# Hybrid decoder trunk on one core: routing places taken per token row, another store order for the rows, and Abs_reciprocal_sqrt in the norms

## The reference

```
def _layer_norm(x, g, b):
    mu = mean(x);  var = mean((x - mu)**2)
    return (x - mu) * rsqrt(var + LN_EPS) * g + b
def _moe_ffn(h, ...):
    scores = sigmoid(h @ w_router);  biased = scores + router_bias      # 64 experts
    keep the 4 best of 8 groups (sum of each group's two best biased scores)
    idx = top_k(biased of the kept groups, 8)
    w = 2.5 * scores[idx] / sum(scores[idx])
    routed = sum over the 8 experts of w * (silu(h Wg) * (h Wu)) Wd
    return routed + shared expert
```

## Time and profile before

| | |
|---|---|
| runs | 1547.74, 1555.4, 1553.97 us; median 1553.97 |
| profiled execution | 1548.17 us; span 1546.3 us from the first to the last instruction |
| PE busy | 1439.7 us (93%) |
| DVE, ACT, POOL busy | 649.5 us, 342.0 us, 244.7 us |
| DMA | 512.37 MB, mean 331 GB/s |
| `norm_and_route` of layer 0, of layer 1 | from 383.9 us to about 411.5; from 1023.6 to about 1052.9 |
| `experts` of layer 0, of layer 1 | from 411.66 us to about 900; from 1053.06 to 1534.7 |

### The profile page before, as it was taken

How to read it: one execution, slowest core, us unless ns; L and a number is a source line. 1 busy time by engine, 2 the same in 40 slices (tenths; PEclk the granted TensorE clock), 3 DMA queues, 4 the chain that set the end, 5 groups by cost and what they waited for, 6 DMA issues and landing times. The chain is left out here.

```text
span 1546.3 us, 24294 instructions
## 1 busy us (share of the span) xinstructions
PE 1439.7 (93%) x9414; PEld 849.9 (55%) x9414; DVE 649.5 (42%) x1461; ACT 342.0 (22%) x712; POOL 244.7 (16%) x323
## 2 busy tenths in 40 slices
PE   8999989999899999897999889989999989979996
PEld 6888768887445545353545467864543333424442
DVE  2767448632632433242433358053234323414324
ACT  3756454220410111010111030141101111101111
POOL 5779625200100000000000000011000000000000
PEclk9999999899999999998999989999999999989998
DMA  8669461049599999999999973498999999999994
GB/s 282 218 190 243 174 173 47 2 164 365 208 417 422 423 420 424 424 421 425 421 425 421 409 281 129 169 392 336 417 424 423 421 425 422 425 421 424 422 423 183
DMA packets 105679, 512.37 MB, mean 331 GB/s; under 512 B 36932, under 2 KB 42116, under 8 KB 68444
## 3 DMA queue, kind: packets, MB, share of 16 engines
q1 hardware_dynamic: 95740, 481.75, 78.7%
q0 software_dynamic: 9824, 29.05, 5.0%
HBM read 508.85 MB, written 17.10 MB: 340 GB/s over the span
## 5 line engine op out<-in xcount | busy, mean ns | idle before, releaser
L1855 PE MATMUL banks<-upper,e_xgT 128*64 128x512 f32 (+1 forms) x880 | 195.1, 609 | 3.5 <-DMA upper<-in_moe_gate_up 2.1
L2064 DVE TENSOR_TENSOR e_ac<-e_sl,banks 128x256 f32<-128x256 f32 x54 | 22.8, 421 | 405.8 <-ACT e_sl L1982 405.8
L346 PE MATMUL banks<-hT,dense_ring 128*128 128x272 f32 x768 | 183.3, 396 | 5.3 <-DMA dense_ring<-in_w_in 5.2
L1444 POOL DMA_INDIRECT x_xg<-rows_dram,x_idx x54 | 53.8, 996 | 824.7 <-DVE x_idx L1436 808.6
L346 PEld LDWEIGHTS banks<-hT,dense_ring 128*128 128x128 f32 x768 | 145.8, 191 | 39.0 <-DMA dense_ring<-in_w_in 5.4
L1855 PE MATMUL banks<-dense_ring,e_xgT 128*64 128x512 f32 (+1 forms) x288 | 134.5, 622 | 34.7 <-issue 34.7
L1855 PE MATMUL banks<-experts,e_xgT 128*64 128x512 f32 (+1 forms) x720 | 159.3, 604 | 1.1 <-DMA experts<-in_moe_gate_up 0.9
L1982 ACT ACTIVATE e_sl<-banks 128x256 f32<-128x256 f32 x54 | 20.8, 385 | 491.2 <-PE banks L1855 491.2
L1855 PEld LDWEIGHTS banks<-upper,e_xgT 128*64 128x64 f32 (+1 forms) x880 | 65.0, 131 | 91.0 <-issue 91.0
L1875 PE MATMUL banks<-x_sg,route_consts 128*128 128x272 f32 x432 | 104.4, 393 | 0.5 <-DVE acc L2051 0.5
L1873 PE MATMUL banks<-route_consts,x_sg 128*128 128x512 f32 x216 | 97.6, 594 | 0.8 <-DVE acc L2048 0.8
(11 more groups left out here) (450 smaller groups left out, 2061.1 us busy)
## 6 DMA issues: line engine op xcount, KB each, us to landing
upper<-in_moe_gate_up SPq DMA_DIRECT2D x45, 2048.0 KB, 27.9
experts<-in_moe_gate_up SPq DMA_DIRECT2D x36, 2048.0 KB, 27.1
upper<-in_moe_down SPq DMA_DIRECT2D x43, 1024.0 KB, 25.5
experts<-in_moe_down SPq DMA_DIRECT2D x43, 1024.0 KB, 26.4
dense_ring<-in_moe_down SPq DMA_DIRECT2D x38, 1024.0 KB, 25.5
dense_ring<-in_moe_gate_up SPq DMA_DIRECT2D x18, 2048.0 KB, 19.1
dense_ring<-in_w_in SPq DMA_DIRECT2D x47, 512.0 KB, 4.8
upper<-in_moe_gate_up SPq DMA_DIRECT2D x20, 1024.0 KB, 15.0
```

Of the source, the lines that this page charges most:

```text
L346: mm = pe.matmul(ps[g % 4][:, 0:T], slot[:, n % SLOTS_IN, c, :], hT[:, c, :], start=(c == 0), stop=(c == DC - 1))
L1444: pool.indirect_dma_start(out=ex["xg"][:, i % 2, :], out_offset=None, in_=mem["rows_dram"], in_offset=bass.IndirectOffsetOnAxis(ap=ex["idx ...
L1855: mm = pe.matmul(gub[e * n:(e + 1) * n, :], xgT[:, i % 2, c, e * n:(e + 1) * n], gate_up_weights(mem, j)[:, c, :], start=(c == 0), stop=(c ...
L2064: dve.tensor_tensor(ac[:], sl[:], gub[:, FF:], ALU.mult).then_inc(mul, 1)
```

## The change

The edits, with what each does:

- In both norms the inverse root comes from one ACT function, `Abs_reciprocal_sqrt`, in place of `Sqrt` and DVE's reciprocal (routing) and of `Ln` and `Exp` (S5 stage). A one-element call of it stands at the start of ACT's list.
- POOL scales the router weights first and clears `x_xg` after the centring.
- ACT does only chunk 0 before the logits' `Sigmoid`, and seven after it.
- Rows are turned, copied and stored with the 16-row tile first (`turn_order`: 2, 0, 1 in layer 0; 0, 1 in layer 1).
- Places are formed by token: PE makes them from `after` and `sel` (six small products in layer 0, three in layer 1), DVE adds 1 and masks, PE turns them to expert rows. DVE takes the maximum from PSUM, ACT then copies the places.
- PE ranks before it spreads; places and gates are spread by separate products, the gates after the sort. DVE's selectors (`select_unit`) come before the scaling, the scatter after the order.

```
 def scalar(act):
+    act.activation(rstd[0:1, 0:1], eps[0:1, 2:3], ACT.Abs_reciprocal_sqrt).then_inc(held, 1)
     for c in range(DC):
         act.wait_ge(centred, c + 1)
         act.activation(sq[:, c, :], hN[:, c, :], ACT.Square).then_inc(squared, 1)
     act.wait_ge(sq_summed, 1)
-    act.activation(rstd[:], sqs[:, 0:T], ACT.Ln, scale=1.0 / D, bias=eps[:, 2:3]).then_inc(logged, 1)
-    act.wait_ge(logged, 1)
-    act.activation(rstd[:], rstd[:], ACT.Exp, scale=-0.5).then_inc(rooted, 1)
+    act.wait_ge(held, 1)
+    act.activation(rstd[:], sqs[:, 0:T], ACT.Abs_reciprocal_sqrt, scale=1.0 / D, bias=eps[:, 2:3]).then_inc(rooted, 1)
...
+turn_order = tuple(range(2, NT)) + (0, 1)
...
-        pool.memset(ex["xg"][:], 0.0).then_inc(ex["xg_zero"], 1)
         pool.wait_ge(loaded, 48 * (layer + 1))
         pool.tensor_tensor(wg[:], wr[:], ln[:, 4 * layer * DC:(4 * layer + 1) * DC].unsqueeze(2).broadcast_to(
             [P, DC, E]), ALU.mult).then_inc(weighed, 1)
-        for tt, (t0, n) in enumerate(tiles):
-            pool.wait_ge(rows_c, NT + tt + 1)
+        pool.wait_ge(centred, DC)
+        pool.memset(ex["xg"][:], 0.0).then_inc(ex["xg_zero"], 1)
+        for i, tt in enumerate(turn_order):
+            t0, n = tiles[tt]
+            pool.wait_ge(rows_c, NT + i + 1)
             pool.dma_start(mem["rows_dram"][t0:t0 + n, :], row_tile(tt)[0:n]).then_inc(stored, 16)
...
-            half, tt = divmod(i, NT)
+            half, tt = i // NT, turn_order[i % NT]
...
         pe.wait_ge(selected, 1)
         for tt, (t0, n) in enumerate(tiles):
-            mm = pe.matmul(rank_ps[0:E, 0:W], sel[0:n, tt, :], after[0:n, tt, 0:W],
-                           start=(tt == 0), stop=(tt == NT - 1))
+            for src, (_, held) in enumerate(tiles[:tt + 1]):
+                mm = pe.matmul(place_ps[0:n, tt * E:(tt + 1) * E], after[0:held, src, t0:t0 + n], sel[0:held, src, :],
+                               start=(src == 0), stop=(src == tt))
+        mm.then_inc(ranked, 1)
+        pe.wait_ge(located, 1)
+        for tt, (t0, n) in enumerate(tiles):
+            mm = pe.transpose(row_places_ps[0:E, t0:t0 + n], sel[0:n, tt, :], ident[0:n, 0:n])
         mm.then_inc(ranked, 1)
         pe.wait_ge(gated, 1)
...
-        pe.wait_ge(placed, 2)
-        pe.wait_ge(rows_c, 2 * NT)
-        for i in range(2):
-            spread_unit(pe, mem, ex, i, spread_ps[i], W)
         pe.wait_ge(mem["expert_consts"], 16 * len(EXPERT_CONSTS))
         pe.wait_ge(keyed, 1)
         pe.matmul(key_ps[0:E, 0:E], ones[0:E, 0:E], keys[:], start=True, stop=True).then_inc(spread, 1)
-        pe.wait_ge(masked, 1)
+        pe.wait_ge(placed, 1)
+        pe.wait_ge(rows_c, 2 * NT)
+        pe.wait_ge(ex["unit_selected"], 2)
+        for i in range(2):
+            pe.matmul(spread_ps[i][0][:, 0:W], ex["selw"][0:E, i], pg[0:E, 0:W], start=True, stop=True).then_inc(
+                ex["rows_broadcast"], 1)
+        pe.wait_ge(placed, 2)
         pe.wait_ge(placed_by, 2)
         pe.matmul(sort_ps[:, 2 * E:2 * E + 1], twice, rank[:], start=True, stop=True)
         pe.matmul(sort_ps[0:1, 0:E], number, at_rank[:], start=True, stop=True)
         pe.matmul(sort_ps[0:1, E:2 * E], cm[:], at_rank[:], start=True, stop=True).then_inc(sorted_, 1)
+        for i in range(2):
+            pe.matmul(spread_ps[i][1][:, 0:W], ex["selw"][E:, i], pg[E:, 0:W], start=True, stop=True).then_inc(
+                gates_spread, 1)
...
+        act.activation(warm[:], eps[0:1, 0:1], ACT.Abs_reciprocal_sqrt).then_inc(warmed, 1)
         for c in range(DC):
             act.wait_ge(centred, c + 1)
             act.activation(sq[:, c, :], hN[:, c, :], ACT.Square).then_inc(squared, 1)
         act.wait_ge(sq_summed, 1)
-        act.activation(rstd[:], sqs[:, 0:W], ACT.Sqrt, scale=1.0 / D, bias=eps[:, 2:3]).then_inc(sd_ready, 1)
-
+        act.activation(rstd[:], sqs[:, 0:W], ACT.Abs_reciprocal_sqrt, scale=1.0 / D, bias=eps[:, 2:3]).then_inc(rooted, 1)
+
+        act.wait_ge(warmed, 1)
         act.activation(warm[:], eps[0:1, 0:1], ACT.Sigmoid).then_inc(warmed, 1)
-        for c in range(3):
-            normal(c)
+        normal(0)
         act.wait_ge(logit_in, 1)
         act.wait_ge(bias_in, 1)
         act.activation(lgT[:], lgT[:], ACT.Sigmoid, bias=bias[:, 0:1]).then_inc(scored, 1)
-        for c in range(3, DC):
+        for c in range(1, DC):
...
-        act.wait_ge(ranked, 2)
-        act.copy(maskT[:], both_ps[0:E, 0:W]).then_inc(masked, 1)
+        act.wait_ge(counted, 1)
+        act.copy(pg[0:E, 0:W], row_places_ps[0:E, 0:W]).then_inc(placed, 1)
+        act.wait_ge(ranked, 3)
         act.copy(pg[E:, 0:W], both_ps[E:, 0:W]).then_inc(placed, 1)
         for i in range(2):
-            gates_in(act, ex, i, spread_ps[i], W)
+            act.wait_ge(gates_spread, i + 1)
+            act.copy(ex["gsb"][:, i], spread_ps[i][1][:, 0:W]).then_inc(ex["gates_in"], 1)
...
+        dve.wait_ge(mem["expert_consts"], 16 * len(EXPERT_CONSTS))
+        fixed = mem["unit_first"]
+        for i in range(2):
+            select_unit(dve, mem, ex, i, fixed[:, len(UNITS) + i:len(UNITS) + i + 1])
         dve.wait_ge(biased, 1)
         dve.tensor_copy(bias[:], bias_ps[0:E, 0:1]).then_inc(bias_in, 1)
-        dve.wait_ge(sd_ready, 1)
-        dve.reciprocal(rstd[:], rstd[:]).then_inc(rooted, 1)
         dve.wait_ge(rooted, 1)
...
+        dve.wait_ge(ranked, 1)
+        dve.scalar_tensor_tensor(out=sel, in0=place_ps[:, 0:NT * E].rearrange("p (t e) -> p t e", t=NT), scalar=1.0,
+                                 in1=sel, op0=ALU.add, op1=ALU.mult).then_inc(located, 1)
...
-        dve.wait_ge(mem["expert_consts"], 16 * len(EXPERT_CONSTS))
-        fixed = mem["unit_first"]
-        for i in range(2):
-            select_unit(dve, mem, ex, i, fixed[:, len(UNITS) + i:len(UNITS) + i + 1])
-        dve.wait_ge(masked, 1)
-
-        dve.scalar_tensor_tensor(out=pg[0:E, 0:W], in0=rank_ps[0:E, 0:W], scalar=1.0, in1=maskT[:],
-                                 op0=ALU.add, op1=ALU.mult).then_inc(placed, 1)
-        dve.wait_ge(placed, 2)
-        link(dve.tensor_reduce(cm[:], pg[0:E, 0:W], AX_X, ALU.max))
+        dve.wait_ge(ranked, 2)
+        dve.tensor_reduce(cm[:], row_places_ps[0:E, 0:W], AX_X, ALU.max).then_inc(counted, 1)
+        dve.wait_ge(counted, 1)
...
-        locate_unit(dve, mem, ex, 0, spread_ps[0], W)
         dve.wait_ge(spread, 1)
...
-        locate_unit(dve, mem, ex, 1, spread_ps[1], W)
         for i in range(2):
-            scatter_unit(dve, mem, ex, i, spread_ps[i], W)
-        link(dve.tensor_scalar(extra[:], rank[:], PAIR_RANKS - 0.5, float(SLOTS // 2), ALU.is_gt, ALU.mult))
+            locate_unit(dve, mem, ex, i, spread_ps[i], W)
         dve.wait_ge(sorted_, 1)
...
-        dve.wait_ge(ex["rows_broadcast"], 2)
-        link(dve.scalar_tensor_tensor(out=pg[0:E, 0:W], in0=maskT[:], scalar=extra[:, 0:1], in1=pg[0:E, 0:W],
-                                      op0=ALU.mult, op1=ALU.add))
+        dve.wait_ge(placed_by, 2)
+        link(dve.tensor_scalar(extra[:], rank[:], PAIR_RANKS - 0.5, float(SLOTS // 2), ALU.is_gt, ALU.mult))
+        link(dve.tensor_scalar(lifted[:], pg[0:E, 0:W], 0.0, extra[:, 0:1], ALU.is_gt, ALU.mult))
+        link(dve.tensor_tensor(pg[0:E, 0:W], pg[0:E, 0:W], lifted[:], ALU.add))
+        for i in range(2):
+            scatter_unit(dve, mem, ex, i, spread_ps[i], W)
```

More of the change, by code:

```diff
@@ L1288, in layer_norm @@
     sq, mean, rstd = sb("ln_sq", [P, DC, T]), sb("ln_mean", [P, T]), sb("ln_rstd", [P, T])
[L1289 to L1290 removed]
+    meaned, centred, squared, sq_summed, held, rooted, scaled, out = (sem(f"ln_{n}") for n in (
+        "meaned", "centred", "squared", "sq_summed", "table_held", "rooted", "scaled", "out"))
     def tensor(pe):
```

16 lines of the change are left out of this document (7 added, 9 removed).

## The result

Kernel after: 1558.05 us median (1552.7 to 1564.88, 9 runs); kernel before, run beside it: 1552.93 us (1547.74 to 1555.4, 9 runs). The ratio is 1.0037, 95% interval [1.0019, 1.0055]: slower by 5.7 us by the ratio (3 to 8.5); the two medians lie 5.1 apart. The forecast was +2.0 us, 1553.3 us in all. The profiled execution took 1558.05 us, its span is 1556.3 us, its mean granted clock 0.961 (0.968 in that of before).

What follows compares the result with a forecast made beforehand. The prediction took the weight stream's start to bound the experts, timed by ACT's rows in layer 0 and PE's chain in layer 1. Layer 0 +1.4, layer 1 +0.6, S5 norm 0: +2.0 on 1551.3 gives 1553.3 us, range 1545 to 1559.

Steps and rivals of the forecast that it cites:

- What bounds the kernel: Expert stages: weights stream at a constant rate, its start timed by ACT's row copies in layer 0, PE's chain in layer 1.
- no gap opens in layer 0: Layer 0's first unit: first two loads last 7.5 us, and the next are asked for halfway through that unit.
- Stream +1.4 us: Layer 0: later selection (0.4) and two moved Identities (1.05) delay last copy, gather and SP's first load by 1.4 us.
- The added table load: Start of ACT's list: 1.28 us, over inside DVE's standstill, so no cost; without that cover 0.5.
- The places' chain at full clock: Layer 0, from `sel` written: gates done at +6.6, shared product at +10.45, PE's first turn at +11.4 against +10.9.
- a clock of 0.5 there: Layer 0's routing: listed among the signs that would show the forecast wrong.
- rival B: Layer 0's clock falls as layer 1's did; first unit 3 us later, a gap opens, about +5, 1556.3 us; chance 0.12.
- forecast at the full clock: Layer 0: PE's first turn comes 0.5 + 0.4 = 0.9 us later, at 412.6.
- The gather's landing: Layer 0: gather moves with the last store and lands at PE's first turn or up to 0.3 us after.
- the sooner order: Layer 0: order known some 0.8 us sooner, which buys nothing while SP waits for the gather.
- Root, S5 norm, tiles first: Layer 0's reciprocal saves nothing; S5 root 1.75 us sooner, hidden by `s_wb`, gain 0; store order -0.4 to +0.3, taken as 0.
- Layer 1 +0.6: Layer 1: shared product starts 1.4 us later but runs less at half clock; +0.6 us, from -0.7 to +1.5.

Runs made afterwards that it cites:

- number 7: Kernel after with SP waiting for both gathers and, as in the kernel before, store order, Identities and POOL's list: 1554.54 us, ratio 1.0021.
- fillers and the wait: Kernel after plus 20 unused products of ones in PE's pauses per routing stage, and SP waiting for both first gathers: 1546.86 us, ratio 0.9963.
- all cures: Kernel after plus filler products, SP waiting for both gathers, three Identities ahead of the sigmoid and POOL's clearing first: 1548.1 us, ratio 0.9973.
- SP's second wait: Kernel after, but SP waits until both first gathers are issued, not one, before loading the first unit's weights: 1554.42 us, ratio 1.0013.
- number 3: Kernel after plus filler products of ones in PE's pauses of both routing stages, nothing else: 1560.59 us, ratio 1.0052.
- 4: Kernel after with SP waiting for both first gathers: alone 1554.42 us, ratio 1.0013; with filler products 1546.86 us, ratio 0.9963.
- number 8: Kernel before with POOL kept busy between the first index and the first gather, so the load follows the gather closely: 1562.68 us, ratio 1.0064.
- places alone: Kernel before with only the new chain of places; root, Identities, store order and POOL's clearing as before: 1555.92 us, ratio 1.0022.
- number 9: The failure: kernel after with fillers and the first unit's index taken ahead of the ranks, without SP's second wait: 1557.43 us, ratio 1.0043.

## Why the prediction was wrong, step by step

- **What bounds the kernel: wrong; this is the step that failed first.** "So layer 0's expert stage is timed by ACT's rows, not by the places", and "so no gap opens in layer 0". The stage is timed by PE's first turn, in layer 0 as in layer 1: from there layer 0 takes 488.0 to 490.5 us in 18 traces. That the DMA engines are never idle at 500 us says nothing of 420 us. The numbers were there: by my own sum the 3 MB were through at 410.3 + 7.5 = 417.8, and a third load as far behind the turn as before (5.8 us) came at 418.4. So I had called a path with no slack hidden, and entered layer 0 with the 1.4 us of ACT's rows in place of what the turn loses.
- **Stream +1.4 us: right for the copies, too much by half for the load, and without effect.** Copies end +1.56 later by the stage's clock (forecast 1.4, the standstill beside POOL and the logits at +10.06 against +9.41 included). SP's load is only 0.7 later, since before it waited for the order, 0.4 us longer than for the gather. Put back (number 7), the earlier copies showed no gain. The added table load took 1.28 us, and ACT's next call started 1.30 us behind its start (384.21 and 385.51), before the first centred chunk was there: no cost, as the sum had it.
- **The places' chain at full clock: right.** From `sel` written to the shared product I had +6.6; with fillers and the wait it took 24.01 - 17.48 = 6.5 us, with all cures 6.6, before 6.0.
- **The clock: the term that was missing.** I left layer 0 at full clock, and named a clock of 0.5 there as a sign of being wrong, which came; rival B had it fall for 3 us of the turn and +5 in all, 1556.3 us, with a chance of 0.12. It fell in every trace of the new chain without fillers: sel to shared product 8.8 us, shared product 6.46, turn 6.0 later than in the one trace of before at full clock, 3.2 later than in the one where it fell there too (forecast at the full clock: 0.9). B was the nearest case, and I had argued against it from one execution, in which the kernel before happened to keep its clock.
- **The gather's landing: not foreseen.** I took the 3.6 us of the kernel before and counted the sooner order as worth nothing. It took SP's last wait away, and the load closed in on the gather from 1.28 and 1.66 us to 0.91 and 0.97 in one execution, to 0.87 and 0.57 in the other. Of the four first gathers in the two traces only one made the turn wait (layer 1, second execution), for 1.2 us; by the ratios, SP's second wait takes away 3.7 us of the 5.7, with intervals that overlap. What the gather costs in this kernel is thus shown in kind (numbers 3, 4 and 8) and not in size.
- **Root, S5 norm, tiles first: right, as far as the runs resolve it.** The logits' product releases DVE, `s_wb` releases the S5 stage, a 512 KB store behind the copies is as good as a 64 KB one; root and tiles alone came to 1.0001 and 1.0004, each with an error of 0.002. DVE's two selectors took 2.10 us beside POOL's clearing (1.89), under the wait for the root; with the clearing elsewhere (places alone) they took 0.47. The Trainium skill, "SBUF — State Buffer", section "Who interferes with whom", lets these two collide, and here the trace agrees.
- **Layer 1 +0.6: too small.** The turn is at +30.5 and +33.3 against +29.4 in both executions before. Over the seven traces of the new chain without fillers it is +30.5 to +33.3, over four of the old chain (number 8 left out) +29.4 to +31.9; the later ones have late rows or an early fall of the clock, for which the sum had no term. The sum also took 0.43 us for a chunk product at the full clock, which is 3.72 / 8 = 0.465.

What stays open: why the gathered rows wait behind the weights (that they do is shown from both sides, the order inside the DMA queues isn't visible), what brings the short falls of the clock at a routing stage's start, why the fillers failed once to keep the clock up (number 9), and how the 5.7 us divide between clock and gather.

## What to carry to other kernels

Find the event whose shift moves the end, over several executions, before costing anything: here a look at what the third load waits for would have shown that it is the first unit's turn. A wait on a queue that never seemed to matter may be what keeps a large transfer behind a small, urgent one; when a change makes it come sooner, look at what then runs side by side. And profile an unstable clock more than once: one execution shows one of its states.

## What the runs showed of the hardware

- The indirect gather of a unit's rows (128 rows of 1024 float32), with a 2 MB load asked for 0.6 us later on another queue, lands in 9.5 to 11.5 us, and in 3.5 to 4.8 us with the load 1.2 us later or more. Gathers issued in the middle of the weight stream take about 10 us. SP's second wait holds the load back by 0.7 us, and with the fillers the kernel is 14 us shorter for it.
- TensorE's granted clock in a stage of small products is not fixed by the program: the same kernel was at 2.4 GHz through a 3.93 us product in one execution, and at 1.2 GHz for most of it in the next, where it took 6.21 us. Twenty products of ones in the pauses of each routing stage took 4.8 us off the kernel before (ratio 0.9969 [0.9952, 0.9986]), and kept the clock up through the shared product in 5 of 6 traces.
- PE waiting with nothing to do loses the clock too: in number 3 the granted clock fell to 0.50 during PE's 4.85 us wait for the rows, and the first unit began at 1.2 GHz.
